# GpSimd makes the upper weight parts of six blocks that ScalarE made, in the recurrent layer's gates

## The reference, cut to what matters

```
def rg_lru(x, w_a, b_a, w_x, b_x, lam):
    xb = x.reshape(bsz, s, N_LRU_BLOCKS, LRU_BLOCK)
    r = jax.nn.sigmoid(jnp.einsum("bsnd,nde->bsne", xb, w_a).reshape(bsz, s, w) + b_a)
    i = jax.nn.sigmoid(jnp.einsum("bsnd,nde->bsne", xb, w_x).reshape(bsz, s, w) + b_x)
    log_a = (-LRU_C * r.astype(jnp.float32)) * jax.nn.softplus(-lam.astype(jnp.float32))
    a = jnp.exp(log_a)
    mult = jnp.sqrt(-jnp.expm1(2.0 * log_a))
    u = mult * (i * x).astype(jnp.float32)
    _, h = lax.associative_scan(combine, (a, u), axis=1)

def recurrent_mixer(...):
    z = hn @ w_in
    gate, xr = jnp.split(z, 2, axis=-1)
    xr = causal_depthwise_conv(xr, conv_w, conv_b)
    y = rg_lru(xr, ...)
    return (y * jax.nn.gelu(gate)) @ w_out
```

## Time and profile before

| | |
|---|---|
| median of 3 runs | 1824.19 us (1821.56 to 1825.34) |
| the profiled execution | 1822.48 us, span 1820.6 us |
| granted TensorE clock, mean | 0.964 |
| busy: TensorE / VectorE / ScalarE / GpSimd | 1685.3 / 1318.5 / 825.1 / 151.3 us |
| DMA | 317.83 MB, 175 GB/s over the span |

### The profile page before, as it was taken

The page is one execution under the profiler, slowest core; times in us unless marked ns, Lnnn a source line. Parts: engine busy times, 40 slices in busy tenths (PEclk is TensorE's granted clock), DMA queues, the critical chain, the costliest instruction groups (busy, mean ns, idle before and its releaser), DMA issues. The chain is left out here.

```text
span 1820.6 us, 28130 instructions
## 1 busy us (share of the span) xinstructions
PE 1685.3 (93%) x11558; PEld 1506.7 (83%) x11558; DVE 1318.5 (72%) x1849; ACT 825.1 (45%) x1185; POOL 151.3 (8%) x155
## 2 busy tenths in 40 slices
PE   5989998999999998799999998957999989789999
PEld 2987776788788877777899997957999979689999
DVE  4695757887978767646677768798898886755543
ACT  3423642533234324435554545564635434446362
POOL 0322000011001100710010100020000000000000
PEclk9999999999999999899999998988999999899999
DMA  9531004233654464310347465536898974125552
GB/s 367 202 139 70 1 24 162 93 139 110 227 229 185 156 222 159 131 47 1 128 148 296 159 246 204 206 112 247 331 350 322 353 271 165 60 93 185 186 176 80
DMA packets 46575, 317.83 MB, mean 175 GB/s; under 512 B 5232, under 2 KB 6256, under 8 KB 12272
## 3 DMA queue, kind: packets, MB, share of 16 engines
q1 hardware_dynamic: 45936, 312.68, 47.5%
q0 software_dynamic: 512, 3.35, 0.5%
HBM read 314.96 MB, written 1.05 MB: 174 GB/s over the span
## 5 line engine op out<-in xcount | busy, mean ns | idle before, releaser
L1523 PE MATMUL PM<-Hhi,whi 128*128 128x256 f32 (+1 forms) x1686 | 527.6, 313 | 23.2 <-DVE Hlo L1369 17.4
L953 DVE TENSOR_TENSOR wlo<-raw,whi 128x2048 fp32r<-128x2048 f32 (+3 forms) x204 | 447.0, 2191 | 130.4 <-ACT whi L661 130.0
L1525 PE MATMUL PM<-Hhi,wlo 128*128 128x256 f32 (+1 forms) x1686 | 522.3, 310 | 0.0
L1524 PE MATMUL PM<-Hlo,whi 128*128 128x256 f32 (+1 forms) x1686 | 522.2, 310 | 0.0
L661 ACT ACTIVATE whi<-raw 128x2048 fp32r<-128x2048 f32 (+3 forms) x204 | 365.2, 1790 | 134.3 <-PE PM L1525 91.1
L1523 PEld LDWEIGHTS PM<-Hhi,whi 128*128 128x128 f32 x1686 | 322.8, 191 | 52.6 <-issue 28.2
L1525 PEld LDWEIGHTS PM<-Hhi,wlo 128*128 128x128 f32 x1686 | 322.8, 191 | 16.5
L1524 PEld LDWEIGHTS PM<-Hlo,whi 128*128 128x128 f32 x1686 | 323.0, 192 | 16.2 <-issue 0.2
L1523 PE MATMUL PM<-Ghi,whi 128*128 128x256 f32 (+1 forms) x864 | 267.6, 310 | 0.8 <-DVE X L1128 0.8
L1525 PE MATMUL PM<-Ghi,wlo 128*128 128x256 f32 (+1 forms) x864 | 263.2, 305 | 0.0
L1524 PE MATMUL PM<-Glo,whi 128*128 128x256 f32 (+1 forms) x864 | 263.2, 305 | 0.0
(11 more groups left out here) (212 smaller groups left out, 2249.2 us busy)
## 6 DMA issues: line engine op xcount, KB each, us to landing
raw<-in_ada SPq DMA_DIRECT2D x104, 1024.0 KB, 4.9
raw<-in_wm SPq DMA_DIRECT2D x93, 1024.0 KB, 5.0
raw<-in_wl SPq DMA_DIRECT2D x68, 1024.0 KB, 5.0
raw<-in_wl SPq DMA_DIRECT2D x32, 704.0 KB, 4.4
raw<-in_wm SPq DMA_DIRECT2D x5, 768.0 KB, 5.6
raw<-in_wm SPq DMA_DIRECT2D x4, 704.0 KB, 4.2
X<-in_x SPq DMA_DIRECT2D x1, 2048.0 KB, 12.8
bias<-in_bias POOLq DMA_DIRECT2D x1, 2048.0 KB, 9.3
```

Of the source, the lines that this page charges most:

```text
L953: dve.tensor_tensor(wslot(wlo, i, usize(u)), slot_raw(n, usize(u)), wslot(whi, i, usize(u)).bitcast(F32), ALU.subtract)\
L1523: pe.matmul(out, st_hi, mv_hi, start=first, stop=False)
L1524: pe.matmul(out, st_hi, mv_lo, start=False, stop=False)
L1525: return pe.matmul(out, st_lo, mv_hi, start=False, stop=last)
```

## The change

GpSimd gets a copy (a cast from float32 to fp32r) of each of the blocks 113 to 118, that is of `lgate` 2 to 5 and `lpart` 0 and 1, with 1536, 1536, 1536, 512, 2048 and 2048 columns. It stands in GpSimd's program at the steps 111 to 116, waits for the load and for `unit` of block i-3 as ScalarE did, and ticks a semaphore of its own. ScalarE leaves these six out. VectorE waits for the new semaphore at them. Nothing else changes: buffers, matmuls, loads and their order are the same.

```
+POOL_HI = [i + 2 for i in range(first_of("lgate", "M0"), first_of("lpart", "M0"))]
...
                 if step[0] == "unit":
                     u = UNITS[step[1]]
                     i = u["i"]
+                    if i + 2 in POOL_HI:
+                        w = i + 2
+                        size = usize(UNITS[w])
+                        raw_ready(pool, ("w", w))
+                        pool.wait_ge(*at("unit", w - SPLIT))
+                        pool.tensor_copy(wslot(whi, w, size), slot_raw(RAW_AT["w", w], size)).then_inc(*tick("hi_pool", w))
...
             def split_hi(i):
 
-                if i >= NU:
+                if i >= NU or i in POOL_HI:
                     return
...
-                dve.wait_ge(*at("hi", i))
+                dve.wait_ge(*at("hi_pool" if i in POOL_HI else "hi", i))
```

More of the change, by code:

```diff
@@ L329, in noted @@
         return self.known.get((name, key), 0)
-SEMAPHORES = ["small", "x_in", "hi", "lo", "raw_used", "unit", "pm_act", "pm_dve", "aux", "aux_act", "aux_dve",
+SEMAPHORES = ["small", "x_in", "hi", "hi_pool", "lo", "raw_used", "unit", "pm_act", "pm_dve", "aux", "aux_act", "aux_dve",
               "silu_c", "mod", "sq", "sumsq", "sd", "rinv", "xr", "hhi", "hlo", "xres",
```

## The result

| | before | changed |
|---|---|---|
| median | 1823.30 us (20 runs) | 1828.56 us (20 runs) |
| ratio, with its 95% interval | | 1.0027 [1.0019, 1.0036] |
| span of the profiled execution | 1820.6 us | 1827.5 us |

A forecast was written before the change was run, and what follows sets the result against it. The prediction took TensorE (busy 93%) as the overall bound, with ScalarE narrowly leading the gates and VectorE next. Its terms 1.55 + 0 + 8.6 - 2.6 gave +7.5 us on 1824.2, so 1831.7 us, range 1827 to 1837.6.

The forecast's parts named there:

- rival A: Gates: casts run near ScalarE's rate, +3.3 us, time 1827.5; sign: scan less than 4 us late; chance 0.17.
- C: Gates: TensorE idles more and its clock falls, +10 us, time 1834; sign: granted clock below 1; chance 0.10.
- First cast: Block 113: copy goes ahead of the `Hlo` pieces, +2.15 us, 0.6 comes back from ScalarE; together +1.55.
- Second cast hidden: Block 114: the 2.15 us copy falls before VectorE's wait of 3.17 us, which hides it; 0.
- Casts of 115 to 118: Gates: 6144 columns at 1.4 ns run beside a VectorE with nothing but work; +8.6 us.
- The price of 1.4 ns per column: GpSimd casts: taken as two thirds of its multiply's 2.1 ns; 2.15 us for 1536 columns.
- the low bound: GpSimd casts: ScalarE's rate, 0.84 ns per column, as the lowest price; sum +3.3 us.
- The four later waits: Gates: VectorE's four later waits for ScalarE go; -2.6 us.
- The new semaphore: Gates: `hi_pool` instead of `hi` costs nothing, as GpSimd is one to two blocks ahead; 0.
- Rival B: Gates: GpSimd stops VectorE only in part or casts fall into its waits; gain stays, 1821 us; chance 0.07.

The follow-up runs named there:

- the run with copies by nobody: The changed kernel with the six GpSimd casts left out and made by no engine; median 1821.85 us, ratio 0.9993.
- filled: The changed kernel plus nine idle matmuls in TensorE's waits ahead of gate blocks 111, 114, 115 and 116; median 1824.83 us, ratio 1.0007.
- the change's second look: The changed kernel unedited, run once more for a second extra profile; 1825.07 us.
- the run with the pad: The kernel before plus one VectorE operation of 2048 columns between the gates and the scan; median 1826.41 us, ratio 1.0018.

## Why the prediction was right, and where it was not

The direction, the range (1827 to 1837.6) and the mechanism held: VectorE's operations stand while a GpSimd cast works on SBUF (2.27 us for 0.69 beside one of 2048 columns), and the casts land on the engine that their removal from ScalarE makes the bound. The size did not: by the prediction's own signs, a scan that starts less than 4 us late is rival A (chance 0.17), and it started 2.23 late. Nor did the `wlo` and the `tensor_scalar` of the gates grow (1.75 and 0.43 us in the change too); it was L1199 that stood. The sign of C, a clock below 1 beside the gate blocks, came in two of the four profiles of the change. That 1828.56 lies in the range is in part luck, since more than half of the 5.3 us between the medians doesn't come from the gates' delay. Term by term, with the measured values:

1. First cast: forecast +1.55. The `Hlo` pieces took 2.24 us for 1.10, so VectorE stood 1.14; TensorE's gap grew by the same 1.14; ScalarE's gates began 0.74 later and VectorE's 0.75, since 0.4 came back from the missing copy. **+0.75.**
2. Second cast hidden: right. It cost VectorE nothing, and itself 3.67 us for waiting.
3. Casts of 115 to 118: forecast 8.6, measured 0.47 + 0.29 + 1.58 + 1.63 = **3.97.** This is the step that failed, by its size. The price of 1.4 ns per column, two thirds of GpSimd's multiply, was too high: 1.90 us for 2048 columns against 1.47 for 1536 is 0.84 ns, ScalarE's own rate, the low bound and rival A's. At that rate the four hold VectorE for 5.2 us at most. Of the 1.2 less, 0.86 fell where VectorE was idle (the cast of 115 ran from 1181.13, VectorE began at 1181.99), and the rest is that VectorE stood a little less than 0.84 ns per column: 1.58 and 1.63 us for 2048 columns, 0.77 to 0.80 ns. The Trainium skill, "GPSIMD Engine Reference", section 4.1, calls GpSimd roughly line-rate on operations with one input; with the 1.03 cycles per element of section 3 that is an estimate of 0.86 ns, and the trace agrees with its 0.84.
4. The four later waits: forecast -2.6. They are gone, and the run with copies by nobody gives -2.49 for the whole relief, the start included.
5. The new semaphore: 0 forecast, no row shows a cost.

The measured terms give 0.75 + 3.97 - 2.6 = 2.1 us, the trace 2.23, the forecast 7.5. So as a statement on the gates the sum was over three times too large. A second effect is real, and the prediction had it as rival C with the wrong place and price (a fall between the later blocks, +10): at the first gate block, whose wait the cast of 113 widened to 2.53 us, a fall of the clock cost 1.5 us in the one profile of the change that has it. It can hardly be the whole of the 2 us by which the mean lies above the gates' delay: it cost less than that, and it was there in one of four profiles. For the same reason the 2.7 us between the means of the filled and the unfilled change hardly all come from the first block, and where they come from is not shown. From the `wlo` of block 111 to the end, the filled profile took 663.2 us, and so did the change's second look, unfilled and without a fall at the first block. The rest of the spread between the profiles lies mainly in the attention of M1 (clock 0.74 twice and 0.83 twice in the change, 59.5 us twice, 56.9 and 56.4). Whether the change makes the longer stretch more frequent stays open: four profiles can't give a frequency.

Rival B (a gain) needed VectorE to have gaps for the casts. As argued, it hadn't once ScalarE was relieved, but for the first wait. With ScalarE's copies kept, the casts used up most of VectorE's later waits (0.15 and 0.46 us are left), and the delay was the same.

## What to carry to other kernels

Before work goes to an idle GpSimd, look at what VectorE does in that stretch: here each column of a cast beside a busy VectorE cost VectorE some 0.8 ns, so only VectorE's waits were free room. When the engine that leads by a little is relieved, the gain is the wait of the next one, here 2.5 us for the 8.8 us of copies taken off ScalarE. And look at a delay ahead of a TensorE block twice where it opens a gap: once for itself, once for the clock that may fall behind it. Idle matmuls in such gaps lowered the mean here, by an amount that the gates alone don't explain, and brought nothing in the kernel before. Last, a time inside the predicted range doesn't confirm the sum: here only the start of the scan showed that its largest term was twice too large.

## What the runs showed of the hardware that was not expected

- A cast from float32 to fp32r on GpSimd runs at 0.84 ns per column of 128 partitions (1.47 us for 1536, 1.90 for 2048), as fast as ScalarE's copy (1.47 and 1.90). It holds VectorE for 0.77 to 0.80 ns per column, GpSimd's multiply of two tensors for 2.1.
- A multiply of 256 columns that takes VectorE 0.40 us cost it 0.54 us by standing still while GpSimd did it: eleven of them moved to VectorE saved 2.09 us of a stretch in which VectorE is busy 21.23 of 22.63 us.
- TensorE waits of 1.7 to 2.5 us were followed by a stretch at the lower clock level in some executions (at 1172 and at 1188 in one profile each of the change) and not in others of the same kernel. With the gates of before, the wait of 1.7 us ahead of block 114 was followed by it in the run with the pad (0.58) and not in the profile of before (1.00).
